# An encoder layer on one core: accumulators cut into 512 + 256 tokens, and one product into two sums for the last 256 tokens

## The reference

```python
h = modulate(rmsnorm(x, norm1_g), sh1, sc1)
proj = h @ w_in                       # q, k, v | Hyena's 3 x 512 | two gates
attn = windowed_gqa_sink(q, k, v, sink)
hy = hyena_branch(proj[...], conv_w, conv_b, spec, hyena_bias)   # width-3 conv, long conv
merged = sigmoid(gate_a) * (attn @ w_attn_o) + sigmoid(gate_h) * (hy @ w_hyena_o)
x = x + g1 * (merged @ w_out)
h = modulate(rmsnorm(x, norm2_g), sh2, sc2)
x = x + g2 * (square(relu(h @ w_up)) @ w_down)                   # d_ff = 4096
y = modulate(rmsnorm(x, final_g), shf, scf)
```

## Time and profile before

| | |
|---|---|
| median of 3 runs | 1123.1 us (1121.71 to 1123.13) |
| span of the profiled execution | 1122.6 us |
| TensorE busy (matmul) | 1092.4 us, 6304 matmuls |
| VectorE busy | 801.6 us |
| ScalarE busy | 452.9 us |
| granted TensorE clock | 90% or more of full speed in all forty slices |

### The profile page before, as it was taken

The page is one execution under the profiler, slowest core; times in us unless marked ns, Lnnn a source line. Parts: engine busy times, 40 slices in busy tenths (PEclk is TensorE's granted clock), DMA queues, the critical chain, the costliest instruction groups (busy, mean ns, idle before and its releaser), DMA issues. The chain is left out here.

```text
span 1122.6 us, 16641 instructions
## 1 busy us (share of the span) xinstructions
PE 1092.4 (97%) x6304; PEld 1020.8 (91%) x6304; DVE 801.6 (71%) x1335; ACT 452.9 (40%) x792; POOL 107.3 (10%) x132
## 2 busy tenths in 40 slices
PE   6989999999999999999999999999999999999996
PEld 4777788888899999999899999999999999999886
DVE  5867689989478685556455777787878778688534
ACT  5631146666632222423346232244342626157414
POOL 2101210000325332000000000000000000000000
PEclk9999999999999999999999999999999999999999
DMA  9932354443342333753312331143333322222303
GB/s 350 389 95 101 150 188 120 136 139 95 110 149 104 104 117 123 266 157 113 112 57 92 119 128 56 56 150 95 113 92 115 95 97 101 86 75 76 94 19 114
DMA packets 45525, 138.85 MB, mean 124 GB/s; under 512 B 5051, under 2 KB 10635, under 8 KB 44556
## 3 DMA queue, kind: packets, MB, share of 16 engines
q1 hardware_dynamic: 29024, 80.21, 21.6%
q0 software_dynamic: 11376, 44.84, 11.5%
q10 hardware_dynamic: 5052, 12.81, 3.3%
HBM read 121.61 MB, written 15.74 MB: 122 GB/s over the span
## 5 line engine op out<-in xcount | busy, mean ns | idle before, releaser
L740 PE MATMUL acc_ps<-act_hilo,w_hi 128*128 128x384 f32 x1536 | 338.2, 341 | 2.4 <-DVE w_lo L1712 1.6
L740 PEld LDWEIGHTS acc_ps<-act_hilo,w_hi 128*128 128x128 f32 x1536 | 269.3, 188 | 22.0 <-issue 20.0
L740 PE MATMUL acc_ps<-act_hilo,w_lo 128*128 128x384 f32 x768 | 195.3, 335 | 0.0
L740 PEld LDWEIGHTS acc_ps<-act_hilo,w_lo 128*128 128x128 f32 x768 | 138.8, 188 | 0.0
L1185 PE MATMUL acc_ps<-hidden_hilo,act_hilo 128*128 128x384 f32 x768 | 135.0, 335 | 0.6 <-DVE hidden_hilo L2274 0.4
L1185 PEld LDWEIGHTS acc_ps<-hidden_hilo,act_hilo 128*128 128x128 f32 x768 | 133.0, 188 | 1.9 <-issue 1.0
L1712 DVE TENSOR_TENSOR w_lo<-w_raw,w_hi 128x1024 fp32r<-128x1024 f32 x62 | 77.0, 1242 | 60.5 <-ACT w_hi L1261 59.6
L1261 ACT ACTIVATE w_hi<-w_raw 128x1024 fp32r<-128x1024 f32 x62 | 65.2, 1052 | 44.5 <-PE acc_ps L740 41.0
L2160 DVE SCALAR_TENSOR_TENSOR xT<-acc_ps,modT,xT 128x512 f32<-128x512 f32 (+1 forms) x32 | 19.7, 617 | 61.4 <-PE acc_ps L819 61.3
L1803 DVE CUSTOM_DVE_ANT_0 dot_out<-dot_ring,c_rows,vecT 128x1024 f32<-128x1024 f32 x48 | 61.6, 1283 | 2.6
L2285 DVE SCALAR_TENSOR_TENSOR xT<-acc_ps,modT,xT 128x384 f32<-128x384 f32 (+2 forms) x96 | 40.5, 478 | 31.4 <-PE acc_ps L1185 31.4
(11 more groups left out here) (292 smaller groups left out, 2006.4 us busy)
## 6 DMA issues: line engine op xcount, KB each, us to landing
w_raw<-in_w_pre SPq DMA_DIRECT2D x50, 512.0 KB, 3.5
dot_ring<-in_w_ada_cols POOLq DMA_DIRECT2D x48, 512.0 KB, 3.8
w_raw<-in_w_up SPq DMA_DIRECT2D x32, 512.0 KB, 4.0
w_raw<-in_w_down SPq DMA_DIRECT2D x16, 512.0 KB, 3.5
w_raw<-in_w_down_half SPq DMA_DIRECT2D x32, 256.0 KB, 2.7
spec<-filt_out POOLq DMA_DIRECT2D x12, 512.0 KB, 3.0
gate_spill<-gates_out ACTq DMA_DIRECT2D x16, 384.0 KB, 2.5
hy_spec<-spec SPq DMA_DIRECT2D x12, 512.0 KB, 5.3
```

Source lines behind the costliest of these rows:

```text
L740: mm = pe.matmul(acc_ps[:, slot, 512 * h:512 * h + HALF], w[:, kw, :], src[:, x, k, HALF * h:HALF * h + HALF], start=(first and i == 0), s ...
```

## The change

The cut of a 768-token tile goes from 384 + 384 to 512 + 256: one bank holds the sample, the first half of the other the prompt. PIECES are two. Where a tile is only added to x (w_down in all its parts and the out projection), the prompt's two passes with the high weight are one matmul of 512 columns, whose moving operand is two pieces (the high and the low parts of 256 tokens) and which writes two sums, at columns 512 to 767 and 768 to 1023 of the slot; the pass with the low weight goes into the first. VectorE adds both sums to x, one after the other, with the sample's piece between them or, in residual_group, with a wait for the first to end. The last tile of each loop over u (u = 15) stays with one sum. Cut to its core:

```diff
-PIECES = ((0, 0, HALF), (0, HALF, TS), (1, TS, T))
+PIECES = ((0, 0, TS), (1, TS, T))
...
+        x_half = cv_part
...
-            return acc_ps[:, s].rearrange("p (h n) -> p h n", n=512)[:, :, 0:HALF]
+            return acc_ps[:, s, 0:T]
         def acc_piece(s, a, b):
-            a, b = (a + 512 - HALF, b + 512 - HALF) if a >= HALF else (a, b)
             return acc_ps[:, s, a:b]
-        def halves(row):
-            return row.rearrange("p (h n) -> p h n", n=HALF)
+        def acc_second(s):
+            return acc_ps[:, s, T:T + TP]
...
-            def gemm_k(slot, s, k, kw, src, first, last):
-                for i, (w, x) in enumerate(((whi[s], 0), (whi[s], 1), (wlo[s], 0))):
-                    for h in range(2):
-                        mm = pe.matmul(acc_ps[:, slot, 512 * h:512 * h + HALF], w[:, kw, :], src[:, x, k, HALF * h:HALF * h + HALF],
-                                       start=(first and i == 0), stop=(last and i == 2))
+            def long_k(slot, hi, lo, k, src, first, last):
+                to = acc_ps[:, slot, 0:TS]
+                for i, (w, x) in enumerate(((hi, 0), (hi, 1), (lo, 0))):
+                    mm = pe.matmul(to, w[:, k, :], src[:, x, k, 0:TS], start=(first and i == 0), stop=(last and i == 2))
                 return mm
+            def short_k(slot, hi, lo, k, src, first, last):
+                to = acc_ps[:, slot, TS:T]
+                for i, (w, x) in enumerate(((hi, 0), (hi, 1), (lo, 0))):
+                    mm = pe.matmul(to, w[:, k, :], src[:, x, k, TS:T], start=(first and i == 0), stop=(last and i == 2))
+                return mm
+            def short_two_k(slot, hi, lo, k, src, first, last):
+                pe.matmul(acc_ps[:, slot, TS:T + TP].rearrange("p (x n) -> p x n", x=2), hi[:, k, :], src[:, :, k, TS:T],
+                          start=first, stop=False)
+                return pe.matmul(acc_ps[:, slot, TS:T], lo[:, k, :], src[:, 0, k, TS:T], start=False, stop=last)
+            def gemm_k(slot, hi, lo, k, src, first, last):
+                a, b = acc_ps[:, slot, 0:TS], acc_ps[:, slot, TS:T]
+                for i, (w, x) in enumerate(((hi, 0), (hi, 1), (lo, 0))):
+                    for to, c0, c1 in ((a, 0, TS), (b, TS, T)):
+                        mm = pe.matmul(to, w[:, k, :], src[:, x, k, c0:c1], start=(first and i == 0), stop=(last and i == 2))
+                return mm
+            def gemm_two_k(slot, hi, lo, k, src, first, last):
+                a, b = acc_ps[:, slot, 0:TS], acc_ps[:, slot, TS:T]
+                for x in range(2):
+                    pe.matmul(a, hi[:, k, :], src[:, x, k, 0:TS], start=(first and x == 0), stop=False)
+                pe.matmul(acc_ps[:, slot, TS:T + TP].rearrange("p (x n) -> p x n", x=2), hi[:, k, :], src[:, :, k, TS:T],
+                          start=first, stop=False)
+                pe.matmul(a, lo[:, k, :], src[:, 0, k, 0:TS], start=False, stop=last)
+                return pe.matmul(b, lo[:, k, :], src[:, 0, k, TS:T], start=False, stop=last)
...
-            def group_k(slot, w, h, k, src, n=None):
+            def group_k(slot, w, h, k, src, n=None, two=True):
                 n = k if n is None else n
-                for i, (w_i, x) in enumerate(((w[0], 0), (w[0], 1), (w[1], 0))):
-                    mm = pe.matmul(acc_ps[:, slot, half(h)], w_i[:, k, :], src[:, x, k, half(h)],
-                                   start=(n == 0 and i == 0), stop=(n == KD - 1 and i == 2))
-                return mm
+                return (long_k, short_two_k if two else short_k)[h](slot, w[0], w[1], k, src, n == 0, n == KD - 1)
             def side_k(s, h, k, src):
-                for i, (w, x) in enumerate(((whi[s], 0), (whi[s], 1), (wlo[s], 0))):
-                    mm = pe.matmul(acc_ps[:, s, 512 * h:512 * h + HALF], w[:, k, :], src[:, x, k, HALF * h:HALF * h + HALF],
-                                   start=(k == 0 and i == 0), stop=(k == KD - 1 and i == 2))
-                return mm
+                return (long_k, short_k)[h](s, whi[s], wlo[s], k, src, k == 0, k == KD - 1)
...
-                    mm = group_k(u % 2, w_out(m), h, k, hid)
+                    mm = group_k(u % 2, w_out(m), h, k, hid, two=u < 2 * KD - 1)
...
-                    mm = gemm_k(s, s, k, k, hid, k == 0, k == KD - 1)
+                    mm = gemm_two_k(s, whi[s], wlo[s], k, hid, k == 0, k == KD - 1)
...
-                    for i, (w, x) in enumerate(((hi, 0), (hi, 1), (lo, 0))):
-                        for h in range(2):
-                            mm = pe.matmul(acc_ps[:, m % 2, 512 * h:512 * h + HALF], w[:, k, :],
-                                           hid[:, x, k, HALF * h:HALF * h + HALF],
-                                           start=(k == 0 and i == 0), stop=(k == PK - 2 and i == 2))
+                    mm = gemm_two_k(m % 2, hi, lo, k, hid, k == 0, k == PK - 2)
...
-                    mm = group_k(s, w_last(m), h, k, hid, n)
+                    mm = group_k(s, w_last(m), h, k, hid, n, two=u < 2 * KD - 1)
...
+            def gated(s, m, gate, g, second):
+                a, b = GROUPS[g][0], GROUPS[g][0] + GROUPS[g][1]
+                src = acc_second(s) if second else acc_ps[:, s, a:b]
+                return dve.scalar_tensor_tensor(xT[:, m, a:b], src, modT[:, gate + m, g:g + 1], xT[:, m, a:b], ALU.mult, ALU.add)
             def residual(s, m, gate, before):
                 if before is not None:
                     dve.wait_ge(acc_free[s], before)
-                for g, a, b in PIECES:
-                    row = xT[:, bass.ds(m, 1), a:b].rearrange("p o n -> p (o n)")
-                    last = dve.scalar_tensor_tensor(
-                        row, acc_piece(s, a, b), modT[:, bass.ds(gate + m, 1), g:g + 1].rearrange("p o n -> p (o n)"),
-                        row, ALU.mult, ALU.add)
-                last.then_inc(acc_free[s], 1)
-            def residual_group(s, m, gate, h):
-                row = xT[:, m, half(h)]
-                dve.scalar_tensor_tensor(row, acc_ps[:, s, half(h)], modT[:, gate + m, h:h + 1], row, ALU.mult, ALU.add)\
-                    .then_inc(acc_free[s], 1)
+                gated(s, m, gate, 1, False).then_inc(x_half, 1)
+                gated(s, m, gate, 0, False)
+                halved[0] += 1
+                dve.wait_ge(x_half, halved[0])
+                gated(s, m, gate, 1, True).then_inc(acc_free[s], 1)
+            def residual_group(s, m, gate, h, two=False):
+                if two:
+                    gated(s, m, gate, 1, False).then_inc(x_half, 1)
+                    halved[0] += 1
+                    dve.wait_ge(x_half, halved[0])
+                gated(s, m, gate, h, two).then_inc(acc_free[s], 1)
+            halved = [len(PIECES) * 12]
             dve.wait_ge(ld_x2, 16)
             dve.wait_ge(dot_done, 2 * DOTS_OUT)
             norm_scale(1)
             for u, (h, m) in enumerate(PART_ORDER):
                 dve.wait_ge(acc_ready, A_OUT + u + 1)
-                residual_group(u % 2, m, G1, h)
+                residual_group(u % 2, m, G1, h, KD <= u < 2 * KD - 1)
...
-                residual_group(u % 2, m, G2, h)
+                residual_group(u % 2, m, G2, h, KD <= u < 2 * KD - 1)
```

29 lines of the change are left out of this document (15 added, 14 removed).

## The result

The changed kernel takes 1128.2 us (median of 10 runs, 1125.0 to 1130.6) where the kernel before took 1123.1 on the same chip (10 runs, 1121.2 to 1125.9): ratio 1.0043, 95% interval 1.0032 to 1.0055. The forecast was 1120.0, a gain; the sign is wrong. The profiled execution took 1127.8 us, with a span of 1125.9.

The account below looks back on a forecast made before the run. TensorE, busy 1092.4 of 1122.6 us, was taken as the bound through product spacing and a few waits. Terms -3.9 + 1.0 + 0.4 - 0.65 = -3.15 us on 1123.1 gave 1120.0 us, range 1118.4 to 1122.6.

Parts of the forecast that it names:

- re-cut, pairs: TensorE's product pairs, 384 + 384 to 512 + 256: 346.7 ns before and after, so zero, 0.5 us either way.
- two sums: w_down: In w_down, one 512-column product replaces two of 256, saving 13.3 ns in each of 64 steps: -0.85 us.
- two sums: st_down: In st_down, the same 13.3 ns saved in 128 steps, less 0.11 us at st_down_pair: -1.6 us.
- VectorE's residual: Adding sums to x takes 1.47 us, 0.28 more in 40 tiles, hidden by VectorE's idle time: cost zero.
- wait at u = 8: In both projections, residual_group's added 0.50 us goes straight into TensorE's wait for the norm's reciprocal: +1.0 us in all.
- side_k: First two up tiles: the wait at k = 7 goes (-0.4 us), the third tile's weight split is less covered (+0.8): +0.4.
- convolution: Short convolution: six VectorE instructions become four, 0.22 us less a tile, gaining 0.65 us where VectorE is the bound.
- A: Rival: the two-piece operand's break costs a start, 13.3 ns, so the two-sum product saves nothing; 1124.0 us, chance 0.10.
- D: Rival: the two-piece operand breaks the stream, making each of 304 products dearer; 1128.1 us at two starts, chance 0.06.
- rival E: TensorE waits for VectorE's longer residual in st_down and w_down, +11 us at most; chance under 0.02.
- B: Rival: VectorE holds back the convolution's gain (+0.65) and u = 13 waits in the out projection (+0.5); 1121.1 us, chance 0.14.
- C: Rival: the added wait at u = 8 is only about 0.1 us each, all else holding; 1119.1 us, chance 0.08.

Follow-up runs that it names:

- two_only: Kernel before with the 512 + 256 cut and two-sum product only in w_down, st_down and tiles 8 to 14 of both projections; 1125.8 us, ratio 1.0031.
- u9: two_only with tile 8 of the out projection and of the last part left at three passes; executed once, 1122.1 us.
- recut_only: Changed kernel without any two-sum product: 512 + 256 everywhere, three passes each; 1127.3 us, ratio 1.0043 to the kernel before.
- contig: Changed kernel with the two-sum product reading one piece of 512 neighbouring columns instead of two of 256; 1127.2 us, ratio 1.0045.
- best: Kernel before plus two-sum product in projection tiles 9 to 14, w_down and st_down tiles 2 to 5, ordered by width, norm spread later; 1121.1 us, ratio 0.9983.
- best_last: best with the new cut in the convolution tiles and three passes again in the out projection; 1120.3 us, ratio 0.9967.
- spread_only: Kernel before with only the norm's spread two steps later in tile 9; median 1121.8 us against 1122.8, ratio 0.9996.
- grouped: Changed kernel with all products of 512 columns first in each step, then those of 256; 1127.3 us, ratio 1.0049.
- recut_again: The same kernel as recut_only, executed once more; 1122.5 us.
- before_again: The kernel before, unchanged, executed once more as the control; 1123.5 us.

## Why the prediction was wrong

By its own steps; measured values are from the three executions of the changed kernel and the runs named.

| step | forecast, us | measured | |
|---|---|---|---|
| re-cut, pairs | 0 (0.5 either way) | +0.5 (294.0-443.0) and, in 2 of 3 executions, +1.6 (merge) | failed |
| two sums: w_down | -0.85 | about +0.1 | failed |
| two sums: st_down | -1.6 | 0, then the wait below | failed |
| two sums: tiles 9 to 14 of the last part | -0.61 | -0.30, in one execution of three -0.61 | half |
| two sums: tiles 9 to 14 of the out projection | -0.61 | -0.23 in two_only, -0.37 in u9 | failed |
| VectorE's residual | 0 | +0.47 in three blocks, 1.4 | failed |
| wait at u = 8 | +0.50 twice | +0.55 twice | right |
| behind that wait | - | +1.55 in 2 of 3 executions (clock) | missing |
| side_k | +0.4 | +0.32 in recut_only (0.66 + 0.53 - 0.87) | right |
| convolution | -0.65 | -0.94 to -1.00 | right, 0.3 short |

**The first failed step** is in the sentences "a pair costs 2 x 173.3 = 346.7 ns now and 226.7 + 120.0 = 346.7 ns after ... I count zero for some 400 steps". Both prices were measured in streams of one width, and I said that the trace has no long stretch with alternating widths, yet bounded the unknown by two sums that say nothing about it. 1 ns in a pair was worth 1.2 us in my own words; it became 0 in some stretches and 6.6 ns in others. Half a microsecond was no bound.

**The second** is "13.3 ns saved" per two-sum step. It is the same mistake again: 4 x 226.7 + 120.0 = 1026.7 ns holds for no step as it was written; it takes 1.042 us. Ordered by width most of it is there (w_down -0.69 of -0.85), so the idea of the change is sound, and its order loses it. Rivals A and D named another cause, the break in the operand; contig excludes it. The sign that I had given for them, a tile of st_down that stays at 4.16 us or grows, came true (4 x 1.042 = 4.17 us), but it can't tell them from a mix of widths. That D's end, 1128.1 us, is all but the measured 1128.2 is chance. The spacing rule of the Trainium skill ("TensorE: Matmul & The Clock Gate", section "Wait — 56ns, not 53.3ns?") gives 2.5 ns over the columns. In no run here did a stream of one width have less than 13.3 ns, so the trace doesn't agree with it; that its result (about nothing) came nearer than mine was by another mechanism.

**The third** is "Cost zero" for VectorE's residual. The idle 2 us before some tiles are real, but I looked at the tiles in the middle of st_down. At its end VectorE and ScalarE go without a break into the chain that makes the hidden halves for the next st_down_pair, and there each late 0.26 us of tiles 6 and 7 is kept: TensorE waits for it 30 us on, behind the Strassen products that lie between. That is rival E, which I gave under 0.02 and priced by tile; its true size is 0.47 us a block. I had asked what comes late only of the slot that the residual frees.

Rivals B and C don't decide: the convolution's gain was there in full, and u = 13's slot came in time; but the out projection had little to win, since the first up tiles wait for VectorE (best against best_last). Two slips of the working change nothing here: A's sum should add back 3.9 us, not 4.05, and the range, from C with 0.5 us for the pairs, starts at 1118.6.

The sum by measured values: -0.97 + 0.50 + 1.05 (merge, mean of three) + 0.26 + 1.03 (clock, 1.55 in two of three) - 0.25 + 0.25 + 1.66 + 2 x 0.55 + 0.07 - 0.07 = +4.6 us, against +5.1 (3.6 to 6.2) in the runs.

**Still open.** Why the alternating stream takes one pace or the other, beyond what it follows; whether the half clock behind tile 9 needs the longer wait; what else the median of recut_only holds beyond its two profiles; and why the runs of nearly all variants, spread_only too, have a lower mean clock (0.9948 to 0.9958) than those of the kernel before (0.9961 to 0.9962; beside best_last it has 0.9956 itself, against 0.9954).

## What to carry to other kernels

A price per product that was read in streams of one size holds for such streams; before a mix of sizes is costed at the sum of its parts, time one, or keep the sizes apart, a tile at a time. Where VectorE's work grows, follow it to the next place at which TensorE waits for that engine, however many stages on, and leave out of the change just those tiles that stand ahead of it. And look at more than one profiled execution of a changed kernel: here the cut alone showed +0.9 us in two profiles and +4 us in its median.

## What the hardware did that I had not expected

- Products of 512 and 256 columns by turns: 346.7 or 353.3 ns a pair, one of the two over a whole stretch; which one, differs between executions in the merge and in st_down, and is the same in all six for eleven single tiles. With three of each width in a row it is 350.0 (grouped). In st_down of recut_only and recut_again that is 62.7 or 63.3 us a block, nothing between.
- Four products of 512 and one of 256: 1.042 us, where the widths by themselves give 1.027.
- One change from narrow to wide and back costs about 20 ns, spread over the first wide products (0.93, 0.91, 0.90 us for four of them).
- Streams of one width repeat to 0.03 us over a stage of 130 us (before_again).
- A wait of 1.27 us between two stretches of products was followed by part of a stretch at 1.2 GHz in four of eight executions, 1.3 to 1.7 us lost each time; a wait of 0.73 us or less at the same place in none of ten. Elsewhere a wait of 1.27 us (at 165 us) had no fall behind it in ten executions, and one of 0.62 us (near 27 us) had one in nine.
